# The first four feed-forward jobs of each layer multiply 128 tokens per product instead of 256

## The reference

```python
for l in range(DEPTH):                      # 2 layers
    u = _rms_norm(x, pre_mix_norm_w[l])
    proj = u @ w_in[l]                      # projections of both branches
    ...
    x = x + _rms_norm(h @ w_out[l], post_mix_norm_w[l])

    u = _rms_norm(x, pre_ffn_norm_w[l])
    f = jnp.square(jax.nn.relu(u @ w_ff1[l])) @ w_ff2[l]     # 1024 -> 4096 -> 1024
    x = x + _rms_norm(f, post_ffn_norm_w[l])
```

## Time and profile before

| | before |
|---|---|
| timed runs | 1072.15 and 1079.12 us, median 1075.63 |
| span of the profiled execution | 1064.2 us |
| PE busy | 1010.9 us, 95% |
| DVE / ACT / POOL busy | 69% / 52% / 13% |
| share of the chain that ended last | PE 91%, DVE 5%, issue 2%, ACT 2%, DMA 1% |
| bytes read | 161.25 MB, 153 GB/s over the span |

### The profile page before, as it was taken

One profiled execution on the slowest core, in us unless ns is written; L12 is line 12 of the kernel. 1 busy time (PEld: TensorE's weight loads), 2 busy tenths in 40 slices (PEclk: granted clock), 3 DMA queues, 4 the chain that ended last, 5 costly groups with the idle time before them and its releaser, 6 DMA issues.

```text
span 1064.2 us, 24113 instructions
## 1 busy us (share of the span) xinstructions
PE 1010.9 (95%) x10552; PEld 987.3 (93%) x10552; DVE 732.4 (69%) x982; ACT 557.7 (52%) x786; POOL 137.9 (13%) x109
## 2 busy tenths in 40 slices
PE   5899899999999899999978999999999989999996
PEld 5899889899999899999978998998999979999995
DVE  6886648698566698745388766677875777886453
ACT  6576365755444554443356753767454445444441
POOL 6201000230000322200010000014000013221001
PEclk9999999999999899999989999999999999999998
DMA  7344424334556176666534443334356544766661
GB/s 252 135 141 158 124 82 130 118 106 149 188 180 197 65 224 192 200 196 195 160 119 135 143 142 121 115 106 121 117 166 189 166 153 145 213 197 199 193 185 40
DMA packets 45608, 163.85 MB, mean 154 GB/s; under 512 B 5184, under 2 KB 5440, under 8 KB 45504
## 3 DMA queue, kind: packets, MB, share of 16 engines
q1 hardware_dynamic: 44928, 161.50, 48.2%
q10 hardware_dynamic: 576, 0.82, 0.2%
HBM read 161.25 MB, written 1.05 MB: 153 GB/s over the span
## 4 chain that ended last, share of the span: by engine, by line
PE 91%; DVE 5%; issue 2%; ACT 2%; DMA 1%; POOL 0%; POOLq 0%; SPq 0%; ACTq 0%; DVEq 0%
PE dense L559 25%; PE dense L560 25%; PE dense L561 24%; DVE wlo L1296 1%; PE sides L945 1%; PE sides L799 1%; PE sides L919 1%; PE sides L920 1%; PE sides L791 1%; DVE utmp L1332 1%; PE sides L955 1%; PE sides L759 1%; PE sides L769 1%; PE sides L895 1%; PE sides L718 1%
## 5 line engine op out<-in xcount | busy, mean ns | idle before, releaser
L1296 DVE TENSOR_TENSOR wlo<-raw,whi 128x1024 fp32r<-128x1024 f32 (+1 forms) x304 | 397.9, 1318 | 195.8 <-ACT whi L973 195.5
L973 ACT ACTIVATE whi<-raw 128x1024 fp32r<-128x1024 f32 (+1 forms) x304 | 315.6, 1047 | 225.7 <-PE dense L561 222.0
L559 PE MATMUL dense<-uh,whi 128*128 128x256 f32 x768 | 223.3, 291 | 5.3 <-DVE wlo L1296 5.3
L560 PE MATMUL dense<-ul,whi 128*128 128x256 f32 x768 | 216.3, 282 | 2.6 <-issue 2.6
L561 PE MATMUL dense<-uh,wlo 128*128 128x256 f32 x768 | 216.3, 282 | 0.0
L559 PEld LDWEIGHTS dense<-uh,whi 128*128 128x128 f32 x768 | 147.2, 192 | 7.8 <-DVE wlo L1296 5.7
L559 PE MATMUL dense<-fuh,whi 128*128 128x256 f32 x512 | 144.3, 282 | 9.9 <-DVE ful L1632 9.6
L561 PEld LDWEIGHTS dense<-uh,wlo 128*128 128x128 f32 x768 | 147.2, 192 | 1.6 <-issue 1.6
L560 PEld LDWEIGHTS dense<-ul,whi 128*128 128x128 f32 x768 | 146.7, 191 | 1.5 <-issue 1.3
L560 PE MATMUL dense<-ful,whi 128*128 128x256 f32 x512 | 143.5, 280 | 0.0
L561 PE MATMUL dense<-fuh,wlo 128*128 128x256 f32 x512 | 143.5, 280 | 0.0
(11 more groups left out here) (289 smaller groups left out, 1923.2 us busy)
## 6 DMA issues: line engine op xcount, KB each, us to landing
raw<-weights SPq DMA_DIRECT2D x304, 512.0 KB, 3.7
xT<-x_t SPq DMA_DIRECT2D x4, 256.0 KB, 5.7
out_t<-xT SPq DMA_DIRECT2D x4, 256.0 KB, 2.3
cst<-consts ACTq DMA_DIRECT2D x1, 512.0 KB, 6.5
prm_all<-params ACTq DMA_DIRECT2D x1, 150.0 KB, 4.0
pos_i<-pos ACTq DMA_DIRECT2D x1, 128.0 KB, 5.5
cst<-consts ACTq DMA_DIRECT2D x1, 6.0 KB, 5.8
```

Source lines behind the costliest of these rows:

```text
L559: mm(o_, h_[:, ws], ahi[:, k0 + k, :], start=is_first, stop=False, skip_group_check=True)
L560: mm(o_, h_[:, ws], alo[:, k0 + k, :], start=False, stop=False, skip_group_check=True)
L973: return A(o_, i_, ACT.Copy)
L1296: TT(wlo[s][:, 0:w], raw[s][:, 0:w], f32(whi[s][:, 0:w]), ALU.subtract).then_inc(lo_ready, 1)
```

## The change

`chunk_products` takes a list of token ranges and runs through the piece once for each. The first four jobs of `ff1` give it two ranges, tokens 0 to 127 and 128 to 255; every other call keeps one range of 256 tokens. Waits for `ful` stand in the first range alone. The bank's start flag is on the first product of the first range, its stop flag on the last of the last.

```diff
-            def chunk_products(bank, n, k0, kcount, cols, ahi, alo, first, last, total_k, need=None):
+            def chunk_products(bank, n, k0, kcount, cols, ahi, alo, first, last, total_k, need=None, token_parts=(slice(0, S),)):
...
-                for k in range(kcount):
-                    if need is not None:
-                        need(k0 + k)
-                    for c in range(nch):
-                        ws = slice(k * cols + c * P, k * cols + (c + 1) * P)
-                        o_ = bank[:, c * S:(c + 1) * S]
-                        is_first = first and k == 0 and c == 0
-                        is_last = last and k == kcount - 1 and c == nch - 1
-                        mm(o_, h_[:, ws], ahi[:, k0 + k, :], start=is_first, stop=False, skip_group_check=True)
-                        mm(o_, h_[:, ws], alo[:, k0 + k, :], start=False, stop=False, skip_group_check=True)
-                        x_ = mm(o_, l_[:, ws], ahi[:, k0 + k, :], start=False, stop=is_last, skip_group_check=True)
+                for part, ts_ in enumerate(token_parts):
+                    for k in range(kcount):
+                        if need is not None and part == 0:
+                            need(k0 + k)
+                        for c in range(nch):
+                            ws = slice(k * cols + c * P, k * cols + (c + 1) * P)
+                            o_ = bank[:, c * S + ts_.start:c * S + ts_.stop]
+                            is_first = first and k == 0 and c == 0 and part == 0
+                            is_last = last and k == kcount - 1 and c == nch - 1 and part == len(token_parts) - 1
+                            mm(o_, h_[:, ws], ahi[:, k0 + k, ts_], start=is_first, stop=False, skip_group_check=True)
+                            mm(o_, h_[:, ws], alo[:, k0 + k, ts_], start=False, stop=False, skip_group_check=True)
+                            x_ = mm(o_, l_[:, ws], ahi[:, k0 + k, ts_], start=False, stop=is_last, skip_group_check=True)
...
-                        r = chunk_products(bank, n, 4 * h_, 4, 256, fuh, ful, h_ == 0, h_ == 1, KD, need1)
+                        r = chunk_products(bank, n, 4 * h_, 4, 256, fuh, ful, h_ == 0, h_ == 1, KD, need1,
+                                           (slice(0, P), slice(P, S)) if i < 4 else (slice(0, S),))
```

## The result

The changed kernel takes 1150.74 us (median of 1146.72 and 1154.76) against 1075.63 us before (1072.15 and 1079.12): ratio 1.0704, 95% interval 1.0645 to 1.0764. The profiled execution has a span of 1152.9 us, its own time is 1154.76.

What follows compares the result with a forecast made beforehand. PE, with 91% of the chain of waits, was taken to bound the kernel. Layer 0's +38.2 and layer 1's +39.2 us gave +77.4, added to 1075.6 for 1153.0 us; the range was 1108 to 1200.

Steps and rivals of the forecast that it cites:

- The price of a narrow product: Jobs 0 to 3 of each layer: the weight load sets 107 ns per 128-token product at full clock, 213 at half.
- The waits: Before job 0 in each layer: the 4.78 us wait for the first block of `ful` stays.
- PE doesn't wait for them today: Blocks 4 to 7 of `ful`: the second token range could cover waits for them, but there are none, so no gain.
- The clock: Jobs 0 to 3: stays at half while only narrow products run; the sum of squares between jobs 1 and 2 raises it.
- After that, jobs 2 and 3 run at full clock: Behind the sum of squares: 192 narrow products at 107 ns, 20.5 us, plus 0.5 us for those before the rise.
- case B: Rival for jobs 0 to 3: weight loads count as activity, clock rises as before; +37.5 us, 1113 us; chance 0.27.
- case A: Main forecast, jobs 0 to 3: half clock until the sum of squares, then full; +77.4 us, 1153.0 us; chance 0.37.
- one fall at 584.4 us: Trace before the change: clock fell after PE idled 1.44 us and ran four products of 40 rows; occupation isn't all.
- The sum: Jobs 0 to 3: layer 0 65.3 us (+38.2), layer 1 64.9 us (+39.2), with 3.3 us for L664 in layer 0's; together +77.4.
- the three fast products: Start of job 0 in layer 1: three products run at full clock before the clock falls, -0.3 us.
- The profiled execution is 11.4 us below the median of the two timed runs for what lies around its span: Whole program: the 1064.2 us span against the 1075.63 us median, used to turn the predicted span into a time.

Runs made afterwards that it cites:

- the same-block experiment: Changed kernel with product and token-range loops swapped, so both 128-token products of a weight block stand together; 1145.48 us (one run).
- the two filling experiments: Dense float32 products in TensorE's wait before job 0: in the changed kernel 1105.47 to 1128.58 us; in the kernel before, also between layers, ratio 0.9993.
- the first experiment: Changed kernel with job 0 kept at 256 tokens per product and jobs 1 to 4 at 128; 1109.04 us, ratio 1.0389.

## Why the prediction was right

**The price of a narrow product.** 107 ns at full clock was taken from L718 (105) and L867 (112). It measured 112 ns, on the side of L867, which is 1 us more in a layer. The prediction says that L718 has the type of weights of these products; it has not, its block is plain float32 and `whi` is fp32r. That the price carried over was shown only by the changed kernel. It also takes the 512 loads of L559 to show that a repeated block is loaded again; L559 comes behind another block each time, and it is the same-block experiment that shows it. At half clock 213 ns was taken from the first load after a wait; it measured (392.83 - 351.84) / 192 = 213 ns. The experiment with half a load shows that the load sets both. The figure of 81 ns from the Trainium skill (TensorE: Matmul & The Clock Gate, "Back-to-back issue gap") doesn't hold for this type: 112 ns.

**The waits.** 4.78 us before the first product in both layers, as before. "PE doesn't wait for them today" is true at half clock only; the two filling experiments show short waits for later blocks of `ful` as soon as job 0 runs at full clock. In the changed kernel, whose job 0 runs at half clock, that didn't matter.

**The clock.** That it stays at half while only narrow products run, and that the sum of squares brings it back, is shown from both sides: with a quarter of those passes it stays down (82.8 us at 0.50), with the passes one job sooner it comes back one job sooner, and with a wide job 0 it is up from there on. The rise lies anywhere from within the passes to 1.4 us behind them, so the prediction's "After that, jobs 2 and 3 run at full clock" holds but for some products. That the weight loads count for it (case B) falls with these: in the 82.8 us one load followed the other almost without a gap (82.62 us of PEld). Case B's time was nearly right for another kernel, the one with the wide job 0 (+39.5 us for B's +37.5). My reason for preferring case A was one fall at 584.4 us, a thin one; it was not tested by itself, so that A came out and not B is in part luck.

**The sum.** Layer 0 was put at 65.3 us and took 65.26. Layer 1 was put at 64.9 and took 66.32: the clock rose 1.2 us into job 2, and was down before job 0 began, so that the three fast products that I had counted weren't there. Together +78.8 for a predicted +77.4. L666 took 2.7 us in layer 0 (392.83 to 395.52) for 3.3, since the clock came back inside it, and jobs 2 and 3 took 21.6 us for 21.0, at 112 ns in place of 107. The two misses cancel, so the agreement to 0.1 us in layer 0 is luck; in layer 1 they don't.

**What was wrong.** "The profiled execution is 11.4 us below the median of the two timed runs for what lies around its span" is no such thing. After the change span and time of one execution are 1152.9 and 1154.76: 1.9 us lie around. The profiled execution of before was a quick one of a kernel whose runs here spread from 1063.5 to 1080.1 us. The step came out even because both medians were taken in the same way. The spans differ by 88.7 us, of which 78.8 are in the changed jobs, 2.9 in jobs 4 to 15 (2.7 of it in layer 1) and 7 in the rest of the program, where nothing was changed. Of these 10 us the trace places 6.0 behind the changed jobs of layer 1. There the 576 products of jobs 4 to 15 start 118 ns apart, where before it was 113, and so do the 768 of the four `ff2` jobs, which take 90.46 us (1050.48 to 1140.94) for 87.15 before (965.11 to 1052.26). From job 0 of `ff2` to the end of the program, before and after:

```profile
965.11:1064.20 99.09, 89.13 (x779) 88.40 (x777) 46.24 (x46) 34.15 (x36) 6.92 (x5) 0.97 0.50 154
1050.48:1152.90 102.42, 92.44 (x778) 91.70 (x776) 46.24 (x46) 34.09 (x36) 6.91 (x5) 0.97 0.47 147
```

A wide product at full clock thus has two paces. The kernel before shows both too (from 355.82 us on 118 ns, in jobs 4 to 15 113 ns), and jobs 4 to 15 take 65.3 us in both layers of the same-block and the early sum of squares, so the slower pace is not a price of the change. What sets it is open, as are the other 4 us; all 10 lie within the spread of single executions.

## What to carry over

A product costs the greater of what it streams and what its weight load takes, and with fp32r and a 128 x 128 block the two meet at 256 columns: 128 and 64 columns were paid for as 256 are (112 and 113 ns). Cutting the moving operand in half doubles the time, whatever order the products are in and even if the block is the same. Half-filled streaming costs a second time where it begins at half clock, because here it didn't bring the clock back (213 ns a product until the sum of squares): put narrow work behind wide work, as in the first experiment. Full-width filling ahead of it, with short waits left, helped in one layer of two. And before the clock is bought back anywhere, look whether another engine is only just in time at half clock.

## What I had not expected

How the same instructions can run at either clock, by how they are entered. 384 narrow products, with the sum of squares behind the first 96, kept the full clock in both layers when a wide job stood ahead of them (44.55 us at 1.00), and 192 stayed at half clock when none did. The 64-column products lost the full clock within 4 us of getting it. And with a filling in place of the wide job, and one wait of half a microsecond ahead of the 128-column products and one among them, the clock fell in one layer of two, which costs 20 us there. By the mean clocks that is also why one program took 1105 us in one run and 1124 to 1129 in the others.
